# Conformer convolution: twelve taps as ScalarE products summed on GpSimd, three on TensorE, sixteen on VectorE

## What is computed

```python
u = x @ conf_w_in + conf_b_in            # 1024 -> 2048
a, g = split(u, 2)
u = a * sigmoid(g)                       # 256 x 1024
c = depthwise_conv_centred(u, conf_dw_w) + conf_dw_b   # 31 taps along the tokens, one filter a feature
c = layer_norm(c, conf_ln_g, conf_ln_b)
y = silu(c) @ conf_w_out + conf_b_out
```

## Time and profile before

| what | value |
|---|---|
| median of 3 runs | 2647.29 us |
| lowest and highest of them | 2640.94 and 2647.49 us |
| the profiled execution's own time | 2638.67 us |
| its span in the trace | 2636.9 us |
| mean granted clock of TensorE | 0.951 |
| busy in the span: PE, PEld | 2352.2 us (89%), 2140.5 us (81%) |
| busy in the span: DVE, ACT, POOL | 1621.3 us (61%), 1115.5 us (42%), 125.9 us (5%) |

### The profile page before, as it was taken

The page is one execution under the profiler, slowest core; times in us unless marked ns, Lnnn a source line. Parts: engine busy times, 40 slices in busy tenths (PEclk is TensorE's granted clock), DMA queues, the critical chain, the costliest instruction groups (busy, mean ns, idle before and its releaser), DMA issues.

```text
span 2636.9 us, 41206 instructions
## 1 busy us (share of the span) xinstructions
PE 2352.2 (89%) x17426; PEld 2140.5 (81%) x17426; DVE 1621.3 (61%) x2650; ACT 1115.5 (42%) x1744; POOL 125.9 (5%) x130
## 2 busy tenths in 40 slices
PE   6998988999879999679998879998999998748998
PEld 3665788998769989679997769996678998747997
DVE  3385455646965554676556466656976655667655
ACT  2424334444264345335334435334545435624433
POOL 0013000000000000000000000004620000000000
PEclk9999998999999999899998879998999999979999
DMA  7337343552135544114543214542034554301551
GB/s 298 112 144 258 142 176 131 189 186 102 65 128 189 183 157 162 62 48 160 184 178 118 96 64 155 182 176 80 1 115 159 190 190 146 130 15 64 192 183 74
DMA packets 50296, 368.33 MB, mean 140 GB/s; under 512 B 5568, under 2 KB 5696, under 8 KB 5824
## 3 DMA queue, kind: packets, MB, share of 16 engines
q1 hardware_dynamic: 49968, 363.59, 38.1%
q10 hardware_dynamic: 144, 2.10, 0.2%
HBM read 364.62 MB, written 1.05 MB: 139 GB/s over the span
## 4 chain that ended last, share of the span: by engine, by line
PE 76%; DVE 15%; ACT 5%; issue 2%; DMA 1%; SPq 0%; DVEq 0%; ACTq 0%
PE psum L225 60%; PE psum L2926 3%; DVE weight_parts L219 2%; PE psum L3581 1%; PE psum L3582 1%; DMA weight_ring<-stream_dram 1%; PE psum L2524 1%; PE psum L3286 1%; DVE work L989 1%; ACT weight_parts L193 1%; PE psum L552 1%; DVE work L3017 1%; DVE work L3018 1%; PE psum L1629 1%; PE psum L3599 1%
## 5 line engine op out<-in xcount | busy, mean ns | idle before, releaser
L225 PE MATMUL psum<-input_parts,weight_parts 128*128 128x256 f32 x8448 | 1032.9, 285 | 59.8 <-DVE input_parts L997 27.0
L225 PEld LDWEIGHTS psum<-input_parts,weight_parts 128*128 128x128 f32 x8448 | 1025.6, 193 | 68.4 <-issue 62.9
L219 DVE TENSOR_TENSOR weight_parts<-weight_ring,weight_parts 128x1024 fp32r<-128x1024 f32 x536 | 631.9, 1220 | 307.8 <-ACT weight_parts L193 306.9
L193 ACT ACTIVATE weight_parts<-weight_ring 128x1024 fp32r<-128x1024 f32 x540 | 541.0, 1051 | 203.4 <-PE psum L225 202.6
L225 PE MATMUL psum<-hidden_parts,weight_parts 128*128 128x256 f32 x3936 | 478.4, 283 | 13.1 <-DVE hidden_parts L2650 6.6
L225 PEld LDWEIGHTS psum<-hidden_parts,weight_parts 128*128 128x128 f32 x3936 | 471.9, 190 | 18.6 <-issue 7.9
L1071 ACT ACTIVATE work<-psum 128x256 f32<-128x256 f32 x132 | 50.6, 384 | 422.0 <-PE psum L225 421.9
L1078 DVE TENSOR_TENSOR work<-work,psum 128x256 f32<-128x256 f32 x132 | 55.6, 421 | 281.8 <-ACT work L1071 281.8
L225 PE MATMUL psum<-work,weight_ring 128*128 128x256 f32 (+1 forms) x608 | 174.1, 445 | 3.5 <-ACT work L544 2.2
L225 PEld LDWEIGHTS psum<-work,weight_ring 128*128 128x128 f32 x608 | 116.8, 194 | 56.6 <-issue 43.9
L2926 PE MATMUL psum<-work 128*128 128x128 f32 x512 | 80.0, 332 | 56.7 <-DVE work L3018 56.7
(11 more groups left out here) (468 smaller groups left out, 2373.9 us busy)
## 6 DMA issues: line engine op xcount, KB each, us to landing
weight_ring<-stream_dram SPq DMA_DIRECT2D x341, 1024.0 KB, 4.8
constants<-constants_dram SPq DMA_DIRECT2D x1, 2176.0 KB, 14.1
work<-s_bc_dram ACTq DMA_DIRECT2D x1, 2048.0 KB, 8.7
work<-ctx_dram SPq DMA_DIRECT2D x1, 1024.0 KB, 8.0
residual<-x_dram SPq DMA_DIRECT2D x1, 1024.0 KB, 10.0
out_dram<-residual SPq DMA_DIRECT2D x1, 1024.0 KB, 3.9
vectors<-vectors_dram SPq DMA_DIRECT2D x1, 550.5 KB, 3.7
constants<-constants_dram SPq DMA_DIRECT2D x1, 65.0 KB, 3.5
```

Of the source, the lines that this page charges most:

```text
L193: act.activation(self.parts[:, s % SPLITS, 0, cols], self.ring[:, i % RING, cols], ACT.Identity)\
L219: ins = dve.tensor_tensor(self.parts[:, s % SPLITS, 1, cols], self.ring[:, i % RING, cols], self.parts[:, s % SPLITS, 0, cols].bitcast(F32 ...
L225: mm = pe.matmul(*args, **kw)
```

## The change

The taps of a chunk are divided anew: 16 on VectorE, 12 as products, 3 on TensorE. ScalarE writes each of the 12 products `u[c]` shifted, times the tap's weight, into an area of its own (`products`, two sets of 12 x 256 columns in turn). GpSimd, which has a `gpsimd` method in this stage now, adds them in four instructions: six pairs at once (1536 columns), then three (768), then one (256), then the last (256) into `total`, each linked to the one before. VectorE adds `total` as a third sum and only then signals `conv_ready[c]`.

The orders change too. TensorE is two projections ahead of its taps: projections 0, 1, 2, taps 0, projection 3, taps 1, and so on. VectorE computes the gate of the next chunk in the middle of its 16 taps. ScalarE makes the tap matrices of a chunk behind its sigmoid, and then its products. New waits: ScalarE for the cleared edges before the first sigmoid, for `ready[c]` and (from the third chunk on) for `summed[c - 2]` before the products of a chunk; GpSimd for the products, and from the third chunk on for `conv_ready[c - 2]` before its last addition; VectorE for `summed[c]` before its last addition.

```diff
--- before.py
+++ after.py
@@ -2468,8 +2468,10 @@
 F_G = F_C + KC * T
 
 
-PE_TAPS = 8
-DVE_TAPS = CONV_C - PE_TAPS
+PE_TAPS = 3
+SUM_TAPS = 12
+DVE_TAPS = CONV_C - PE_TAPS - SUM_TAPS
+F_PROD = 17408
 
 
 class ConformerIn(Stage):
@@ -2492,16 +2494,20 @@
         self.gated = k.counter("conf_gate").events(KC)
         self.ready = k.counter("conf_u").events(KC)
         self.conv_ready = k.counter("convolved").events(KC)
+        self.prod = k.area(F_PROD, 2, SUM_TAPS, T)
+        self.total = k.area(F_PROD + 2 * SUM_TAPS * T, 2, T)
+        self.prod_ready = k.counter("conf_products").events(KC)
+        self.summed = k.counter("conf_summed").events(KC)
         self.jobs, self.tap_jobs = [], []
-        for c in range(KC + 1):
+        for c in range(KC + 2):
             if c < KC:
                 self.jobs.append(k.job(self.ready[c]))
-            if c >= 1:
-                self.tap_jobs.append(k.job(self.conv_ready[c - 1]))
+            if c >= 2:
+                self.tap_jobs.append(k.job(self.conv_ready[c - 2]))
 
     def tensor(self, pe):
         k = self.k
-        for j in range(KC + 1):
+        for j in range(KC + 2):
             if j < KC:
                 job = self.jobs[j]
                 begin(pe, job)
@@ -2514,13 +2520,13 @@
                                               slab[:, c, half * P:(half + 1) * P], self.x[:, c, :],
                                               start=(c == 0), stop=(c == KC - 1))
                 mm.then_inc(job.full[0], 1)
-            if j >= 1:
-                c, job = j - 1, self.tap_jobs[j - 1]
+            if j >= 2:
+                c, job = j - 2, self.tap_jobs[j - 2]
                 begin(pe, job)
                 pe.wait_ge(*self.taps_ready[c])
                 pe.wait_ge(*self.ready[c])
                 for i in range(PE_TAPS):
-                    at = DVE_TAPS + i
+                    at = DVE_TAPS + SUM_TAPS + i
                     mm = pe.matmul(job.ap[:, 0:T], self.taps[:, c % 2, i, :], self.u[:, c, at:at + T],
                                    start=(i == 0), stop=(i == PE_TAPS - 1))
                 mm.then_inc(job.full[0], 1)
@@ -2532,20 +2538,44 @@
             act.wait_ge(*self.tap_jobs[c - 2].full)
         for i in range(PE_TAPS):
             ins = act.activation(self.taps[:, c % 2, i, :], k.c("ident"), ACT.Identity,
-                                 scale=k.v("conf_dw_w", (DVE_TAPS + i) * KC + c))
+                                 scale=k.v("conf_dw_w", (DVE_TAPS + SUM_TAPS + i) * KC + c))
         ins.then_inc(self.taps_ready[c][0], 1)
 
+    def products(self, act, c):
+
+        k = self.k
+        act.wait_ge(*self.ready[c])
+        if c >= 2:
+            act.wait_ge(*self.summed[c - 2])
+        for i in range(SUM_TAPS):
+            at = DVE_TAPS + i
+            ins = act.activation(self.prod[:, c % 2, i, :], self.u[:, c, at:at + T], ACT.Identity,
+                                 scale=k.v("conf_dw_w", at * KC + c))
+        ins.then_inc(self.prod_ready[c][0], 1)
+
     def scalar(self, act):
         k = self.k
-        self.make_taps(act, 0)
+        act.wait_ge(*self.edges)
         for j, job in enumerate(self.jobs):
             act.wait_ge(*job.full)
             if j >= 2:
                 act.wait_ge(*self.ready[j - 2])
             act.activation(self.gate[:, j % 2, :], job.ap[:, T:2 * T], ACT.Sigmoid,
                            bias=k.v("conf_b_in", KC + j)).then_inc(self.gated[j][0], 1)
-            if j + 1 < KC:
-                self.make_taps(act, j + 1)
+            self.make_taps(act, j)
+            self.products(act, j)
+
+    def gpsimd(self, pool):
+        link = self.k.pool.link
+        for c in range(KC):
+            p = self.prod[:, c % 2, :, :]
+            pool.wait_ge(*self.prod_ready[c])
+            link(pool.tensor_tensor(p[:, 0:6, :], p[:, 0:6, :], p[:, 6:12, :], ALU.add))
+            link(pool.tensor_tensor(p[:, 0:3, :], p[:, 0:3, :], p[:, 3:6, :], ALU.add))
+            link(pool.tensor_tensor(p[:, 0, :], p[:, 0, :], p[:, 1, :], ALU.add))
+            if c >= 2:
+                pool.wait_ge(*self.conv_ready[c - 2])
+            pool.tensor_tensor(self.total[:, c % 2, :], p[:, 0, :], p[:, 2, :], ALU.add).then_inc(self.summed[c][0], 1)
 
     def vector(self, dve):
         k = self.k
@@ -2559,6 +2589,8 @@
             for j in range(DVE_TAPS):
                 w = k.v("conf_dw_w", j * KC + c)
                 src, acc = self.u[:, c, j:j + T], sums[j % 2]
+                if j == DVE_TAPS // 2 and c + 1 < KC:
+                    self.gate_chunk(dve, c + 1)
                 if j == 0:
                     ins = dve.tensor_scalar(acc, src, w, k.v("conf_dw_b", c), ALU.mult, ALU.add)
                 elif j == 1:
@@ -2566,13 +2598,12 @@
                 else:
                     ins = dve.scalar_tensor_tensor(acc, src, w, acc, ALU.mult, ALU.add)
                 k.dve.step(ins, behind=1)
-            if c + 1 < KC:
-                self.gate_chunk(dve, c + 1)
             dve.wait_ge(k.dve.sem, k.dve.count)
             k.dve.link(dve.tensor_tensor(sums[0], sums[0], sums[1], ALU.add))
             dve.wait_ge(*self.tap_jobs[c].full)
-            dve.tensor_tensor(sums[0], sums[0], self.tap_jobs[c].ap[:, 0:T], ALU.add)\
-               .then_inc(self.conv_ready[c][0], 1)
+            k.dve.link(dve.tensor_tensor(sums[0], sums[0], self.tap_jobs[c].ap[:, 0:T], ALU.add))
+            dve.wait_ge(*self.summed[c])
+            dve.tensor_tensor(sums[0], sums[0], self.total[:, c % 2, :], ALU.add).then_inc(self.conv_ready[c][0], 1)
 
     def gate_chunk(self, dve, c):
 
```

## The result

| what | before | after |
|---|---|---|
| median of 6 runs | 2647.39 us | 2678.31 us |
| lowest and highest | 2640.94 and 2657.16 us | 2673.02 and 2687.01 us |
| the profiled execution's own time, its span | 2638.67, 2636.9 us | 2673.16, 2671.3 us |
| ratio after / before | | 1.0123, 95% interval [1.0104, 1.0143] |

The kernel became 31 us slower; the forecast was 2676 us. Through the document a *stage* is the time from the first projection's start to the start of the copy of the first mean (`self.rs`, line 2642 before, 2673 after), and a *period* is the time from the gate of chunk 3 to that of chunk 7, divided by four. Before: stage 717.77 - 626.89 = 90.9 us, period 10.33. After: 754.07 - 630.85 = 123.2 us, period 13.62.

A forecast was written before the change was run, and what follows sets the result against it. Before, TensorE's chain bounds at 10.36 us a chunk, VectorE nearly full. After, VectorE 7.75 plus GpSimd 6.22 make 13.97 us; the stage ends 28.8 us later, profiled 2638.67 to 2667.5, by the median 2676 us, range 2652 to 2690.

The forecast's parts named there:

- The exclusion: Convolution stage: GpSimd's additions and VectorE instructions with two SBUF inputs take turns, one whole instruction at a time; chance 0.75.
- the sum: Convolution stage: VectorE's and GpSimd's times laid end to end, 13.97 us a chunk, with corrections; stage from 635.1 to 745.8.
- GpSimd's hold: Convolution stage: four additions of 6.74 us, each less 0.13 us, exclude VectorE for 6.22 us a chunk.
- VectorE's own chunk: Convolution stage, VectorE alone: 10.08 us less 2.77 for seven fewer taps, plus 0.44 for the added sum: 7.75 us.
- The moved gate costs the same in its new place: VectorE's gate, moved among the taps: no added cost, and ScalarE's products start half a chunk early.
- The wait for the edges: First sigmoid's new wait on ScalarE: costs nothing, as clearing is over at 629.36 and the projection comes at 634.
- the fast rival: No turn-taking between additions and taps: TensorE bounds at 8.21 us a chunk, 10.4 us less than before; chance 0.12.
- No exclusion: Rival: an addition leaves VectorE's second input free, both engines run at their own pace; 2637 by the median; chance 0.12.
- The half hold: Rival: an addition excludes VectorE for about half its time; 10.9 us a chunk, +7, 2654 by the median; chance 0.10.
- TensorE did go down to 1.2 GHz: Rival: TensorE at 1.2 GHz through the stage, 16.4 us a chunk as the bound, +38, 2685; chance 0.03.
- The 16 matmuls behind the stage: Norm behind the stage: 5.42 us, perhaps 6.9 at 1.2 GHz, up to 1.5 us more, kept only for the range.
- VectorE keeps its turn: Rival inside the main case: GpSimd gets in only at gate, sums and waits; stage end 742 to 750; no own chance.

The follow-up runs named there:

- run 3: The change without GpSimd's second and third additions (1536 and 256 columns left); period 11.61 us, stage 105.4 us, executed once.
- run 12: The change without GpSimd's first three additions (only the last, 256 columns, left); period 8.44 us, stage 83.0 us, executed once.
- run 7: The change with ScalarE's wait for the cleared edges moved from the first sigmoid to the first products; stage 120.2 us, ratio to before 1.013.
- run 8: The change's new orders with the old division (8 taps TensorE, 23 VectorE, no products, no GpSimd); stage 98.3 us, ratio to before 1.0034.
- run 9: New orders and old division, no GpSimd, but TensorE only one projection ahead of its taps; stage 94.3 us, ratio to before 1.0015.
- run 5: The change with VectorE's two accumulators in a free PSUM bank, sums reordered, nothing left out; stage 83.7 us, ratio to before 0.9974.
- run 4: The change with GpSimd's same sums made in eleven additions of 256 columns instead of four; period 12.78 us, stage 117.3 us, executed once.
- run 2: The change with GpSimd's additions replaced by memsets (fifteen of 512 columns, one of 256); period 9.33 us, stage 92.4 us, executed once.

## Why the prediction was right, and where it was off

**The exclusion** was the step that everything hung on, and it held: read in two rows of another stage, with copies on 32 partitions and 512-column taps, it gave the size for additions on 128 to within 5% (5.92 us a chunk for 5.66). From the first gate's end to the last convolved chunk the sum had 745.8 - 635.1 = 110.7 us; measured 110.6 (642.1 to 752.76). Period forecast 13 to 14.3, measured 13.62; mean tap over 700 ns, measured 872, the longest 3.66 us, ending 0.27 us behind an addition where 0.3 was forecast; GpSimd's 256-column additions 786 ns; TensorE under 70% busy from 690 on (67% from 700, 49% from 730), though still 81% and 84% in the two windows from 670, while it ran ahead; products 4.90 / 12 = 0.41 us; the gate and the PSUM add 477 and 420 ns.

**Two terms were off and cancelled, which is luck.** GpSimd's hold was taken as its duration less 0.13 us, with 0.3 us a chunk hidden under the gate: 5.92 us. It is the duration less 0.27 for each addition, 5.66 (runs 3, 12 and the change agree): the runs show the size, not the reason. Taken whole, as the Trainium skill has it (page "SBUF — State Buffer", section "Who interferes with whom"), the durations would be 6.74; here the measurement decides. And VectorE's own chunk is 7.97 us, not 7.75. "The moved gate costs the same in its new place" was the step that failed: before, it stood between the last tap and the first sum and covered the wait between them. Now that wait is bare: the first sum starts 0.58 us behind the start of the last tap (670.09 and 669.51), where a step from tap to gate or from gate to sum is 0.40. That is nearly the whole 0.22.

**The wait for the edges** I had costed at nothing, by its length. It cost 1.28 us by where it stands, through the table load (run 7). The question to ask of it was what else comes between this wait and the instruction that is late.

**The total.** The forecast was a rise of 28.7 us at the median; measured 30.9. The table load and the longer first projections of the profiled execution, 3.0 us together, are not in the sum. The step from one execution to the median was luck too: the one profiled before lay 8.6 us under its median, the one after 5.2, and it had 4.0 us more ahead of the stage.

**The order.** I gave the earlier projection no price of its own. In the change it costs nothing visible, since the additions hold VectorE longer; with the old division it costs 4.1 us (runs 8 and 9), and the gate's place 2.8 (by the trace of run 9). It would have counted in the fast rival, where TensorE's first taps were in the sum (649.15).

**The rivals.** No exclusion: run 5 comes near that case, 2637.47 us median against 2645.34 of before on the same chips. That is 7.9 us less, where the rival had 10.4 (2637 from 2647.29), so it had the direction and about the size; that the two medians agree is chance. The half hold falls by run 3. TensorE did go down to 1.2 GHz (0.50 in the window from 730), and nobody waited for it, so that rival falls too. The 16 matmuls behind the stage, for which 1.5 us were allowed, took 5.38 us for 5.42; the lower clock cost 0.5 us in the two matmuls ahead of them. That VectorE keeps its turn does not happen: in the change as in run 4 one tap is let through at each addition.

## What to carry to other kernels

Before work goes to GpSimd, ask where VectorE's second input lies. A GpSimd instruction that reads SBUF and a VectorE instruction with two SBUF inputs nearly add up in time, and cutting them finer changes that little; here, with the accumulators in PSUM, they overlapped whole. The tensor_scalar form from SBUF to SBUF waits as well, for additions and even for memsets (runs 4 and 2). And a free engine is no cover: look in another stage of the same trace for the two engines at work together, and compare one instruction's duration there with the same form alone.

## What had not been expected of the hardware

- The price of a turn: an addition of GpSimd beside VectorE's taps costs VectorE its duration less 0.27 us, for the mixtures of 256, 768 and 1536 columns in runs 3, 12 and the change, while GpSimd loses 0.06 us by a tap between two of its additions. Eleven short ones cost less (4.8 us a chunk) than four that do the same sum (5.65).
- A GpSimd memset leaves the multiply-add with two SBUF inputs alone (472 ns) and holds up the tensor_scalar form from SBUF to SBUF: 0.3 us for one of 512 columns (run 2), 2 us for one of 4096.
- A tap with its accumulator in PSUM is no slower (481 ns), but tensor_scalar that writes PSUM takes 541 and 477 ns where it takes 407 and 347 to SBUF.
- Where a table load stands in ScalarE's queue depended on whether one or two waits were written ahead of the activation: with two, one wait is an instruction of its own (L2560) and the load came behind it. Why the load is not put ahead of both is open.
